# Mixer out projection: the forgetting half of the next tile is turned ahead of this tile's products, both halves share one PSUM bank, the last tile has banks of its own

## What is computed

```python
o_fox = head_rms_norm(forgetting_attention(fq, fk, fv, log_f), g_fox_out)      # columns 0 to 511
o_gla = head_rms_norm(gla_chunked(gq, gk, gv, log_a), g_gla_out)               # columns 512 to 1023
o_gla = o_gla * jax.nn.silu(z[..., OFF_GR:IN_WIDTH])
y = concatenate([o_fox, o_gla]) @ w_out
x = x + rms_norm(y, g_mix_post)
h = rms_norm(x, g_mem_pre)             # what the memory attention reads
```

## Time and profile before

| | us |
|---|---|
| median of 3 runs | 2402.02 |
| lowest and highest | 2401.54, 2402.18 |
| profiled execution, its own time | 2414.85 |
| its span, first to last instruction | 2413.0 |
| TensorE busy in the span | 2291.6 (95%) |
| VectorE, ScalarE, GpSimd busy | 1097.9, 773.1, 476.1 |
| out projection, end of tile 0 to end of tile 7 | 1242.6 to 1392.8 |

### The profile page before, as it was taken

One profiled execution on the slowest core, in us unless ns is written; L12 is line 12 of the kernel. 1 busy time (PEld: TensorE's weight loads), 2 busy tenths in 40 slices (PEclk: granted clock), 3 DMA queues, 4 the chain that ended last, 5 costly groups with the idle time before them and its releaser, 6 DMA issues. The chain is left out here.

```text
span 2413.0 us, 27043 instructions
## 1 busy us (share of the span) xinstructions
PE 2291.6 (95%) x10640; PEld 1862.5 (77%) x10640; DVE 1097.9 (45%) x1356; ACT 773.1 (32%) x1210; POOL 476.1 (20%) x447
## 2 busy tenths in 40 slices
PE   5999999999999999999999899989799999999997
PEld 4788888788877787778777687758588888878886
DVE  7444444364455334452244443234844444445446
ACT  6333333321223523331222243333533333332113
POOL 3444443200021000000221100001344434320003
PEclk9999999999999889999998999989899999999999
DMA  3222222343342000011121152022122222233323
GB/s 118 83 87 70 87 95 80 109 136 96 114 115 71 11 19 19 19 27 53 61 88 53 44 175 87 18 87 88 53 70 87 88 87 88 70 128 125 110 91 122
DMA packets 105823, 194.94 MB, mean 81 GB/s; under 512 B 8113, under 2 KB 73666, under 8 KB 102882
## 3 DMA queue, kind: packets, MB, share of 16 engines
q1 hardware_dynamic: 105698, 193.21, 24.9%
HBM read 153.28 MB, written 39.91 MB: 80 GB/s over the span
## 5 line engine op out<-in xcount | busy, mean ns | idle before, releaser
L1314 PE MATMUL ps<-xc,wg 128*128 128x512 f32 x1232 | 485.2, 394 | 29.4 <-DVE xc L1828 21.3
L1315 PE MATMUL ps<-xc,wg 128*128 128x512 f32 x1232 | 483.5, 392 | 0.0
L1316 PE MATMUL ps<-xc,wg 128*128 128x512 f32 x1232 | 483.0, 392 | 0.0
L1314 PEld LDWEIGHTS ps<-xc,wg 128*128 128x128 f32 x1232 | 234.0, 190 | 81.0 <-issue 22.5
L1332 PE MATMUL ps<-d_w,d_hid 128*128 128x512 f32 x704 | 276.2, 392 | 7.2 <-DVE y L1867 7.2
L1333 PE MATMUL ps<-d_w,d_hid 128*128 128x512 f32 x704 | 275.8, 392 | 0.0
L1334 PE MATMUL ps<-d_w,d_hid 128*128 128x512 f32 x704 | 275.5, 391 | 0.0
L1316 PEld LDWEIGHTS ps<-xc,wg 128*128 128x128 f32 x1232 | 233.8, 190 | 49.3
L1315 PEld LDWEIGHTS ps<-xc,wg 128*128 128x128 f32 x1232 | 234.1, 190 | 48.5
L1834 DVE TENSOR_TENSOR wg<-w_sums,wg 128x1024 fp32r<-128x1024 f32 x88 | 124.7, 1417 | 188.7 <-ACT wg L830 188.7
L1870 DVE TENSOR_TENSOR y<-y,ps 128x1024 f32<-128x1024 f32 x88 | 107.5, 1221 | 216.1 <-PE ps L1334 216.1
(11 more groups left out here) (266 smaller groups left out, 3856.6 us busy)
## 6 DMA issues: line engine op xcount, KB each, us to landing
w_raw<-in_w_ff_gate SPq DMA_DIRECT2D x22, 1024.0 KB, 6.6
w_raw<-in_w_ff_up SPq DMA_DIRECT2D x22, 1024.0 KB, 5.4
hid_dram<-hid SPq DMA_DIRECT2D x22, 1024.0 KB, 4.6
raw<-hid_dram SPq DMA_DIRECT2D x44, 512.0 KB, 3.8
raw<-in_w_ff_down SPq DMA_DIRECT2D x44, 512.0 KB, 3.7
raw<-in_w_mix_in SPq DMA_DIRECT2D x24, 512.0 KB, 3.9
x_row<-x_dram SPq DMA_DIRECT2D x24, 512.0 KB, 4.2
x_dram<-x_ring SPq DMA_DIRECT2D x16, 512.0 KB, 4.9
```

The costliest lines, as they stand in the source:

```text
L1314: mm(acc, hi, x_hi, start=STARTS[q] and k == 0, stop=False, skip_group_check=True)
L1315: mm(acc, hi, x_lo, start=False, stop=False, skip_group_check=True)
L1316: last = mm(acc, lo, x_hi, start=False, stop=k == 3, skip_group_check=True)
```

## The change

- `o_t` becomes three buffers: `o_t_f` for the forgetting half, two of them by the parity of the tile, and `o_t_g` for the gated half. `turned_half(i, b)` picks one.
- Both halves are turned into bank 3. `turn_o(i, b)` waits for the `low_o` just before its own; `gla_first` waits for none, since bank 0 is its own now.
- In the loop, `turn_o(i + 1, 0)` stands ahead of the products of tile `i`; `turn_o(i + 1, 1)` stands right behind them, and both `gla_out` of tile `i + 2` behind that.
- On ScalarE and VectorE the copy and the remainder of the forgetting half move to the head of the round; those of the gated half stand ahead of `square1` and `scale_y`.
- The last tile writes banks 0 and 1 (`out_bank`), and waits for the readers of these and not for `scale_y`. The query products change pairs of banks.
- In the loop ahead, the forgetting half of tile 0 is turned one product earlier.

```diff
         head_gain = small("head_gain", [P, KT])
-        o_t = [at_kb(f"o_t{a}", 136 + 4 * a, [P, KT, P], F32R) for a in range(2)]
+        o_t_f = [[at_kb(f"o_t_f{i}{a}", (136, 168)[i] + 2 * a, [P, 4, P], F32R) for a in range(2)] for i in range(2)]
+        o_t_g = [at_kb(f"o_t_g{a}", 140 + 2 * a, [P, 4, P], F32R) for a in range(2)]
...
         def out_bank(bd, i):
-            return 2 if bd == 3 and i % 2 else 4
+            if bd == 2:
+                return 0 if i == NT - 1 else 4
+            return 2 if i % 2 else 4
+
+        def turned_half(i, b):
+            return o_t_g if b else o_t_f[i % 2]
...
             def high_o(i, b):
                 act.wait_ge(o_turned, 2 * i + b + 1)
-                wait(act, rows_done, i)
-                sc.activation(o_t[0][:, 4 * b:4 * b + 4, :], cols4(ps[:, 3 - 3 * b, :]), ACT.Copy).then_inc(o_t_hi, 1)
+                wait(act, rows_done, i if b else i - 1)
+                sc.activation(turned_half(i, b)[0][:, :, :], cols4(ps[:, 3, :]), ACT.Copy).then_inc(o_t_hi, 1)
...
             for i in range(NT):
                 if i + 1 < NT:
+                    high_o(i + 1, 0)
                     square_g(i + 1)
-                    high_o(i + 1, 0)
+                    high_o(i + 1, 1)
                 square1(2, i)
-                if i + 1 < NT:
-                    high_o(i + 1, 1)
                 if i > 0:
                     high_h(2, i - 1)
                 square2(2, i)
...
             for c in range(2):
-                keep_mq(c, 0, c)
+                keep_mq(c, 0, 2 + c)
...
                     pe.wait_ge(state_done, 2 * i)
-                    wait(pe, o_t_lo, 2 * i - 2)
                 for s in range(2):
...
             def turn_o(i, b):
                 if b:
                     pe.wait_ge(o_normed, i + 1)
-                    pe.wait_ge(att_kept, min(i + 2, NT))
                 else:
                     pe.wait_ge(f_normed, i + 1)
-                wait(pe, o_t_lo, 2 * i - 1 + b)
+                wait(pe, o_t_lo, 2 * i + b)
                 src = o_tile[i % 2][:, HT:D] if b else S[:, i, 0:HT]
                 for k in range(4):
-                    last = nc.tensor.transpose(ps[:, 3 - 3 * b, tile_of(k)], src[:, tile_of(k)], ident[:, :])
+                    last = nc.tensor.transpose(ps[:, 3, tile_of(k)], src[:, tile_of(k)], ident[:, :])
...
             def out_tile(bd, i, o, w):
 
-                if bd == 2 or i < 2:
+                if bd == 2 and i == NT - 1:
+                    pe.wait_ge(att_kept, NT)
+                    pe.wait_ge(state_done, 2 * NT - 1)
+                elif bd == 2 or i < 2:
                     wait(pe, t1_done, 8 * (bd - 1) + (i if bd == 2 else 0))
...
-                if i == 5:
-                    for b in range(2):
-                        turn_o(0, b)
+                if i in (4, 5):
+                    turn_o(0, i - 4)
...
             for i in range(NT):
                 if i + 2 < NT:
                     gla_first(i + 2)
                 pe.wait_ge(o_t_lo, 2 * i + 2)
-                pe.wait_ge(d_lo_done, S_0 + S_MQ)
-                out_tile(2, i, o_t, lambda a, k, h: (h_hi, h_lo)[a][:, 4 * h:4 * h + 4, tile_of(k)])
                 if i + 1 < NT:
                     turn_o(i + 1, 0)
-                if i + 2 < NT:
-                    gla_out(i + 2, 0)
+                pe.wait_ge(d_lo_done, S_0 + S_MQ)
+                out_tile(2, i, lambda k: [t[:, k % 4, :] for t in turned_half(i, k // 4)],
+                         lambda a, k, h: (h_hi, h_lo)[a][:, 4 * h:4 * h + 4, tile_of(k)])
                 if i + 1 < NT:
                     turn_o(i + 1, 1)
                 if i + 2 < NT:
-                    gla_out(i + 2, 1)
+                    for s in range(2):
+                        gla_out(i + 2, s)
                 if i > 0:
                     turn(2, i - 1)
...
             for c in range(2):
-                mq(c, 0, c)
+                mq(c, 0, 2 + c)
             turn(2, NT - 1)
-            mq(0, 1, 2)
+            mq(0, 1, 0)
...
             for i in range(NT):
                 if i + 1 < NT:
+                    low_o(i + 1, 0)
                     sum_g(i + 1)
                 if i + 2 < NT:
                     keep_att(i + 2)
                     next_state(i + 2)
                 if i + 1 < NT:
                     norm_g(i + 1)
-                    low_o(i + 1, 0)
+                    low_o(i + 1, 1)
                 scale_y(2, i)
-                if i + 1 < NT:
-                    low_o(i + 1, 1)
                 if i > 0:
                     low_h(2, i - 1)
                 make_row(2, i)
```

More of the change, by code:

```diff
@@ L1197, in _ @@
                     square_g(0)
-                if i == 5:
-                    for b in range(2):
-                        high_o(0, b)
+                if i in (4, 5):
+                    high_o(0, i - 4)
             for i in range(NT):
                 if i + 1 < NT:
+                    high_o(i + 1, 0)
                     square_g(i + 1)
-                    high_o(i + 1, 0)
+                    high_o(i + 1, 1)
                 square1(2, i)
-                if i + 1 < NT:
-                    high_o(i + 1, 1)
                 if i > 0:
@@ L1219, in _ @@
             high_s(S_MK)
-            keep_mq(0, 1, 2)
+            keep_mq(0, 1, 0)
             for b in range(4):
@@ L1223, in _ @@
             high_s(S_MK + 1)
-            keep_mq(1, 1, 3)
+            keep_mq(1, 1, 1)
             for k in range(2, 16):
@@ L1554, in out_tile @@
                     for k in range(KT):
-                        last = three(ps[:, out_bank(bd, i) + h, :], [t[:, k, :] for t in o], [w(a, k, h) for a in range(2)],
+                        last = three(ps[:, out_bank(bd, i) + h, :], o(k), [w(a, k, h) for a in range(2)],
                                      k == 0, k == KT - 1)
@@ L1727, in _ @@
             for c in range(2):
-                mq(c, 0, c)
+                mq(c, 0, 2 + c)
             turn(2, NT - 1)
-            mq(0, 1, 2)
+            mq(0, 1, 0)
             for b in range(4):
                 turn_mem(b)
-            mq(1, 1, 3)
+            mq(1, 1, 1)
             for k in range(KT):
@@ L1742, in _ @@
                 pe.wait_ge(d_lo_done, S_0 + NS)
-                out_tile(3, i, mo_t[i % 2], lambda a, k, h: mo_w[a][:, k, half(h)])
+                out_tile(3, i, lambda k: [t[:, k, :] for t in mo_t[i % 2]], lambda a, k, h: mo_w[a][:, k, half(h)])
                 if i > 0:
@@ L2065, in low_o @@
                 dve.wait_ge(o_t_hi, 2 * i + b + 1)
-                hi, lo = (t[:, 4 * b:4 * b + 4, :] for t in o_t)
-                ve.tensor_tensor(lo, cols4(ps[:, 3 - 3 * b, :]), f32(hi), ALU.subtract).then_inc(o_t_lo, 1)
+                hi, lo = (t[:, :, :] for t in turned_half(i, b))
+                ve.tensor_tensor(lo, cols4(ps[:, 3, :]), f32(hi), ALU.subtract).then_inc(o_t_lo, 1)
             def norm_mem(j):
@@ L2203, in _ @@
                     sum_g(0)
-                if i == 5:
-                    for b in range(2):
-                        low_o(0, b)
+                if i in (4, 5):
+                    low_o(0, i - 4)
             norm_f(NT - 1)
```

## The result

The changed kernel took 2378.05 us as the median of 4 runs, against 2402.1 us for the kernel before (4 runs): 0.9896 of it, with a 95% interval of 0.9864 to 0.9929. It is faster by 1%, and lies inside the stated range, 6.55 us above the forecast. The four runs do not scatter around 2378: they are 2369.1, 2371.2, 2384.9 and 2386.3 us. These two levels are most of what is left to explain. The traced execution, at 2386.29 us, is of the upper one. Five other runs in this document, two of warm_before, two of few_fill and one of the kernel before, had a clearly lower clock throughout (0.955 to 0.961, 2422 to 2449 us) and are left out of every number.

The account below looks back on a forecast made before the run. TensorE was taken to be bound by out projection waits for `low_o` and the lowered clock. 32.3 us saved less 1.8 for a new wait gave 30.5 off the 2402.02 us median: 2371.5 us, range 2367 to 2381.

Parts of the forecast that it names:

- the sum: Out projection, end of tile 0 to tile 7, rebuilt from pieces at full clock: 117.87 us against 150.19.
- steps (a) to (c): Rounds: products need no wait for `scale_y`; after a tile's end (T), gated `low_o` ends at 1.96 us, `norm_g` at 13.8.
- The new wait: Second gated half waits on TensorE's queue for the first's end (`og_done`): 0.3 us a round, 1.8 in six.
- The h row: Turning an h row on TensorE in an out projection round: 0.79 us.
- The two turns: Turning the forgetting and gated halves on TensorE in each round: 0.44 and 0.49 us.
- The last tile: With its own banks it waits only for its gated `low_o`, starting 2.11 us after the previous tile's end.
- Its share: Clock loss in the out projection, taken as regained with the pauses: 17.6 us of 32.3.
- rival 1: Clock in the out projection falls all the same, every round (2389 us) or about half (2380); chance 0.13.
- The row of 850 to 860 us: Sign for the clock falling anyway: attention stage busy 10.00 of 10.00 us without a pause, at clock 0.50.
- the forecast's own 2375: Upper end of the main forecast's own span for the whole kernel, 2368 to 2375 us, chance 0.78.

Follow-up runs that it names:

- warm_before: Kernel before plus 12 extra products, results unread, at the start of the first pair of attention heads: 2403.33 us.
- few_fill: Changed kernel plus 4 + 2 extra unread products at the start of the attention and 4 in the round after tile 0: 2371.86 us.
- warm_swap: Kernel before plus 12 extra attention products and, of the change, only the new order on ScalarE and VectorE: 2379.76 us.
- behind: Changed kernel plus 12 extra attention products, with gated copy and remainder back behind `square1` and `scale_y`: 2382.63 us.
- again: Changed kernel, not edited, run six more times: 2370.79 us.
- between: Changed kernel with the gated turn put between the two halves of `gla_out`, no longer ahead of both: 2367.88 us.
- warm_after: Changed kernel plus 12 extra unread products at the start of the first pair of attention heads: 2375.68 us.
- old_last: Changed kernel plus 12 extra attention products, with the last tile back in banks 4 and 5, waiting for `scale_y`: 2378.94 us.
- turn_first: Changed kernel with the next forgetting half turned ahead of the scores and states (`gla_first`), no longer behind them: 2368.49 us.
- both: turn_first with the gated turn also put between the two halves of `gla_out`: 2369.45 us.

## Why the prediction was right

**The wait and its place.** Right: L1504 waits no longer, nothing took its place in a full round, and `low_o`, `scale_y` and `norm_g` end where the sum put them. The steps (a) to (c) needed no correction: the products of tile 6 start at T + 4.90 without a wait (predicted 4.66). What the prediction missed is that the list order on ScalarE and VectorE alone does most of the work (warm_swap), and so does the rest of the change without it (behind). It treated the bank and the order as one cause.

**The stage.** The sum said 117.87 + 1.8 = 119.7 us. Measured 119.9 where the clock held (again). Inside, terms were off and cancelled, which is luck. The new wait was put at 0.3 a round and is 0.21 (between), 1.3 in six rounds and not 1.8. The h row was put at 0.79 us, from a place where products follow; ahead of `gla_first` it takes 1.02 (1283.97 to 1284.99), 0.23 more in each of the four rounds that have this pair, 0.9 in all. The two turns together are 0.08 shorter a round than their terms (0.44 and 0.41 us for 0.49 and 0.44). The last tile came at T + 2.01.

**The clock.** Its share was taken as wholly regained. That is so in `again`, where the stage has 1.00. In the traced execution of the changed kernel it falls once, in the round after tile 0:

```profile
1244.85 0.71 PE L1507 MATMUL ps<-S 64*128 64x128 f32 x4
1245.48 0.65 PE L1514 MATMUL ps<-S 64*64 64x128 f32 x8
1246.07 1.07 PE L1507 MATMUL ps<-S 64*128 64x128 f32 x4
1247.06 1.12 PE L1514 MATMUL ps<-S 64*64 64x128 f32 x8
1248.11 1.11 PE L1546 MATMUL ps<-ident,S 128*128 128x128 f32 x4
```

L1507 and L1514 take 0.71 and 0.65 us the first time, 1.07 and 1.12 the second, with no pause in front. This is rival 1, in one round and at 3.1 us; the prediction gave it 0.13 for all rounds or half of them, and nothing for one alone. Five traced executions leave the work of this round as the change has it (changed, again, warm_after, old_last, behind); in four of them the clock fell in it, in again it did not. The rows show what sets this round apart: no h row stands between `gla_out` and `gla_first`. The five kernels that have other work in it, or a turn at another place (turn_first, few_fill, between, both and also warm_swap, 17.65 us), did not lose the clock in this round, nor did the later rounds of the changed kernel, with the h row. The time of its start does not set it apart: the clock fell with the round starting at 1228.2 us (warm_after) and held at 1228.0 (few_fill). That fits the order of the work as the cause; with one trace of each kernel, and again as the exception, it is not proven. The row of 850 to 860 us was the sign for it. The Trainium skill ("TensorE: Matmul & The Clock Gate", section "What's actually happening") has the low clock after idleness; this round does not agree either, with TensorE busy for 20.53 of 20.60 us at 0.83.

**From the traced execution to the median.** This is the step that failed in part. The prediction found 12.8 us between the traced execution of before and its median and carried them over as they stood, without asking in which stage they lay, as if all runs of a kernel were alike. They are a state of the attention stage: half clock from 830 to 862 us in the trace, and by its times in 7 of 36 runs of before and in 4 of 10 of the changed kernel. The gain taken over whole was right on the common level, 2400.6 to 2369.9, which is 30.7 against the 30.5 that were predicted; on the other it is 2412.8 to 2385.3, 27.5; the missing 3.2 would be the round after tile 0, which lost 3.1 in the upper trace and nothing in the lower, one trace on each level (in warm_after it was lost with the attention at full clock, so the two do not always go together). The median of four runs, two on each level, fell between them at 2378. It lies above the forecast's own 2375, and the range held it since its upper end had been stretched to 2381 for rival 1; most of the distance came from another stage. That is luck: single runs on the upper level (2384.8 to 2386.3) lie outside the range, and one more of them among the four would have put the median there.

## What to carry to other kernels

A remainder or copy that feeds TensorE goes ahead of a chain that has to wait for other engines on the same queue; four lines of order brought 21.0 of the 26.6 to 29.8 us of the whole change. Over the stage the 15 us of pause that went took about as much lost clock with them, but not pause by pause: before the change 1.56 us ahead of tile 6 cost no clock, 4.61 us ahead of tile 7 cost 2.1 us. Before a sum is made against one traced execution, look for a stretch that holds half clock while TensorE is busy: it may be there in some runs and not in others, and at 12 us it was here nearly half the gain. When pieces of a round are put together in a new order, take each piece's length from a place where the same piece follows.

## What the runs showed of the hardware

TensorE's clock stayed low, and once fell, without any pause. The stretch from 830 to 862 us was busy for 32.00 of 32.00 us at a mean clock of 0.52 in one execution, and at 1.00 for 31.48 in another, of the same program; pauses of 0.73 and 0.33 us stand just ahead of or at its start in both. In the round after tile 0 the clock fell with TensorE busy for 20.53 of 20.60 us. Whether the long stretch was lost went, in twelve traces of twelve, with whether the clock had fallen some 30 us before it: where it had (0.81 or 0.91 from 788 to 806 us), it held later.

Twelve extra full products (2.7 us) at the start of that stretch stand in five traces, all with 1.00 there, and the time up to tile 0 was 10.0 to 13.0 us shorter than in the traces at half clock. But five traces without the twelve, one of them with six, have 1.00 too. Since most runs hold the clock by themselves, the median gained nothing: 2403.33 us in ten runs against 2401.36 in the 16 of the kernel before beside them.

How much clock a pause costs did not go by its length alone. The 48 products behind it took 11.01 us after a pause of 1.56 us (before, tile 6) and 12.57 after 1.68 (warm_swap, the same tile). Ahead of the last tile they took 12.34 after 3.20 (old_last), 13.87 after 3.25 (warm_swap), 12.61 after 4.11 (behind) and 13.12 after 4.61 (before).
